# Two transformer blocks on one Trainium2 core: norms summed by token column or inside the next unit's products, a new order of the last two retention heads, and GpSimd multiplying the neighbourhood attention's probabilities

## The reference, cut to what matters

```python
# block 1
x = x + rmsnorm(token_mixer(rmsnorm(x, norm_mix_pre), ...), norm_mix_post)
x = x + rmsnorm(cross_attention(rmsnorm(x, norm_cross_pre), rmsnorm(mem, mem_norm), ...), norm_cross_post)
x = x + rmsnorm(conv_glu_ffn(rmsnorm(x, norm_ffn_pre), ...), norm_ffn_post)
# block 2: an even and an odd layer
x = x + even_mixer(rmsnorm(x, attn_norm_e), ...)   # window attention and neighbourhood attention, 8 heads each
x = x + mlp0(rmsnorm(x, mlp_norm[0]))              # square(relu(h @ w1)) @ w2, width 4096
x = x + odd_mixer(rmsnorm(x, ret_norm_o), ...)     # retention, 8 heads, both directions
x = x + mlp1(rmsnorm(x, mlp_norm[1]))

def rmsnorm(x, g):      # over the 1024 features of each token
    return x * rsqrt(mean(x * x, axis=-1) + 1e-6) * g
# neighbourhood attention, per head and query row
p = softmax(where(valid, q @ k.T * scale + bias, -inf));  o = p @ v
# odd mixer, after retention: per-head group norm, then the gate
y = (silu(g) * groupnorm(y)) @ w_out
```

## Time and profile before

| | |
|---|---|
| median of 3 runs | 2315.23 us (2314.81 to 2315.4) |
| the profiled execution's own time | 2315.41 us |
| its span, first to last instruction | 2313.6 us |
| mean granted TensorE clock | 0.976 of full speed |
| TensorE matmul busy | 2187.5 us, 95% |
| VectorE, ScalarE, GpSimd busy | 1042.4, 854.1, 815.4 us |

### The profile page before, as it was taken

One profiled execution on the slowest core, in us unless ns is written; L12 is line 12 of the kernel. 1 busy time (PEld: TensorE's weight loads), 2 busy tenths in 40 slices (PEclk: granted clock), 3 DMA queues, 4 the chain that ended last, 5 costly groups with the idle time before them and its releaser, 6 DMA issues.

```text
span 2313.6 us, 26996 instructions
## 1 busy us (share of the span) xinstructions
PE 2187.5 (95%) x9972; PEld 1724.4 (75%) x9972; DVE 1042.4 (45%) x1528; ACT 854.1 (37%) x1275; POOL 815.4 (35%) x343
## 2 busy tenths in 40 slices
PE   6889998989999988998999999999999988999999
PEld 5766676758888865765788888788878766888887
DVE  5556646485534363357432312335742665322121
ACT  5334544432222242446442322435432433433231
POOL 3322224224444432220344444443333323444443
PEclk9899999989999999999999999999999999999999
DMA  4212112113322341110222322322222212323223
GB/s 148 66 53 74 64 64 91 64 54 106 123 95 96 100 136 55 64 46 1 83 98 93 100 93 98 107 91 72 75 68 81 80 46 73 97 95 100 95 97 101
DMA packets 54967, 193.36 MB, mean 84 GB/s; under 512 B 6096, under 2 KB 6352, under 8 KB 54480
## 3 DMA queue, kind: packets, MB, share of 16 engines
q1 hardware_dynamic: 50400, 181.58, 24.0%
q10 hardware_dynamic: 4464, 10.36, 1.4%
HBM read 189.82 MB, written 2.10 MB: 83 GB/s over the span
## 4 chain that ended last, share of the span: by engine, by line
PE 73%; issue 13%; DVE 9%; POOL 3%; ACT 2%; DMA 0%; POOLq 0%; SPq 0%; DVEq 0%; ACTq 0%
PE gemm_ps L500 22%; PE gemm_ps L501 21%; PE gemm_ps L502 21%; POOL wl L469 3%; PE out_ps L908 2%; DVE tmp L1654 1%; DVE arena L2022 1%; DVE tmp L2029 1%; PE turn_ps L695 1%; DVE arena L1654 1%; PE score_ps L686 1%; DVE x L1676 1%; PE out_ps L705 1%; DVE xl L1654 1%; PE score_ps L900 1%
## 5 line engine op out<-in xcount | busy, mean ns | idle before, releaser
L469 POOL TENSOR_TENSOR wl<-raw,wh 128x1024 fp32r<-128x1024 f32 x339 | 815.2, 2406 | 1480.4 <-ACT wh L1137 1480.3
L500 PE MATMUL gemm_ps<-xh,wh 128*128 128x512 f32 x1512 | 612.9, 405 | 44.2 <-DVE xl L1654 24.8
L1137 ACT ACTIVATE wh<-raw 128x1024 fp32r<-128x1024 f32 x339 | 359.0, 1059 | 774.5 <-DMA raw<-w_in 745.6
L501 PE MATMUL gemm_ps<-xl,wh 128*128 128x512 f32 x1512 | 593.3, 392 | 0.0
L502 PE MATMUL gemm_ps<-xh,wl 128*128 128x512 f32 x1512 | 593.3, 392 | 0.0
L501 PE MATMUL gemm_ps<-arena_r,wh 128*128 128x512 f32 (+1 forms) x1124 | 433.0, 385 | 0.0
L500 PEld LDWEIGHTS gemm_ps<-xh,wh 128*128 128x128 f32 x1512 | 286.9, 190 | 125.7 <-issue 46.9
L500 PE MATMUL gemm_ps<-arena_r,wh 128*128 128x512 f32 (+1 forms) x868 | 335.5, 387 | 10.8 <-DVE arena_r L1659 10.1
L501 PEld LDWEIGHTS gemm_ps<-xl,wh 128*128 128x128 f32 x1512 | 287.2, 190 | 65.5 <-issue 7.9
L502 PE MATMUL gemm_ps<-arena_r,wl 128*128 128x512 f32 (+1 forms) x868 | 333.3, 384 | 0.0
L502 PEld LDWEIGHTS gemm_ps<-xh,wl 128*128 128x128 f32 x1512 | 286.5, 189 | 61.0
(11 more groups left out here) (334 smaller groups left out, 2011.1 us busy)
## 6 DMA issues: line engine op xcount, KB each, us to landing
raw<-w_in SPq DMA_DIRECT2D x339, 512.0 KB, 3.3
arena<-na_in ACTq DMA_DIRECT2D x14, 256.0 KB, 2.7
x<-x_in SPq DMA_DIRECT2D x8, 256.0 KB, 6.6
out<-x ACTq DMA_DIRECT2D x8, 256.0 KB, 2.8
arena<-alibi_in ACTq DMA_DIRECT2D x6, 256.0 KB, 3.3
con<-con_in SPq DMA_DIRECT2D x1, 1432.0 KB, 11.9
arena<-moba_in ACTq DMA_DIRECT2D x1, 1024.0 KB, 5.1
arena<-mem_in ACTq DMA_DIRECT2D x1, 1024.0 KB, 4.8
```

What stands on the lines that cost most here:

```text
L469: pool.tensor_tensor(wl[:, k, :], raw[:, k, :], wh[:, k, :].bitcast(F32), ALU.subtract).then_inc(unit_split, 1)
L500: pe.matmul(o, wh[:, n % RING, w], h[:, kt, 0:width], start=(kt == 0), stop=False)
L501: pe.matmul(o, wh[:, n % RING, w], l[:, kt, 0:width], start=False, stop=False)
L1137: act.activation(wh[:, k % RING, :], raw[:, k % RING, :], ACT.Copy).then_inc(high_split, 1)
```

## The change

1. *Post-norms by token* (`token_norm`, `inverse_tokens`): the sum of squares goes to 128x4 (token within a tile of 128, by tile), root and reciprocal are taken of 128x4, and four matmuls spread the result over turn_ps bank 1, which `add_normed` now reads in PSUM. For the mixer's and the cross attention's output the last blocks are squared by ScalarE from PSUM, before or beside VectorE's copy.
2. *Pre-norms after an add* (`whole_sum`): the sum stands inside the first unit, after its block kt = 5, and VectorE adds all 8 squares.
3. *Memory units*: `memory_scaled(b)` follows `add_normed` of block b.
4. *Odd order* (`HEAD_STEPS`): the units of heads 6 and 7 are permuted; the last head's two gate units stand beside its own retention steps 0 and 1, head 6's two gate units two places later than head 7's first two. `odd_out1`'s first two units are begun at steps 3 and 4.
5. *Neighbourhood attention*: VectorE stops after the reciprocal; GpSimd multiplies (32 operations), between wl of `even_out`+2 and of `even_out`+3.

```diff
+HEAD_STEPS = [[(h, u) for u in range(U_HEAD)] for h in range(RH - 2)]
+HEAD_STEPS.append([(RH - 2, 0), (RH - 2, 1), (RH - 2, 2), (RH - 2, 3), (RH - 1, 0), (RH - 1, 1)])
+HEAD_STEPS.append([(RH - 1, 2), (RH - 1, 3), (RH - 2, 4), (RH - 2, 5)])
+HEAD_STEPS.append([(RH - 1, 4), (RH - 1, 5)])
+        token_std, token_rstd = eps[:, 4:8], eps[:, 8:12]
+        spread_rstd = turn_ps[:, 1, :]
 # GpSimd
+            beside = FIRST["even_out"] + 3
+            lower_units(0, beside)
+            for i, it in enumerate(pair_items("neighbour")):
+                pool.wait_ge(inverse_ready, i + 1)
+                a = 12 * (i % 3) + 8
+                for s in range(2):
+                    p = pair_probs(i, s, it["nk"], False)
+                    m = pool.tensor_scalar(p, p, small[:, a + s:a + s + 1], None, ALU.mult)
+                m.then_inc(probs_ready, 1)
+            lower_units(beside, UNITS)
 # TensorE
+                    if after is not None and kt == nkt - 3:
+                        after()
+            def whole_sum():
+                take(square_added, KT - 1)
+                pe.matmul(turn_ps[:, 0, :], ones, square_sum, start=True, stop=True).then_inc(square_used, 2)
+            def token_sums(squares, first, last):
+                for c in range(T):
+                    col = CCOL["col"] + 4 - c
+                    m = pe.matmul(turn_ps[:, 0, 0:T], squares[:, c * P:(c + 1) * P], con[:, col:col + T],
+                                  start=(first and c == 0), stop=(last and c == T - 1), skip_group_check=True)
+                return m
+            def token_norm(apart=1):
+                take(square_added, KT - 1 - apart)
+                token_sums(square_sum, True, False)
+                if apart == 2:
+                    take(square_made, KT - 1)
+                    token_sums(sq[:, (KT - 2) % 2, :], False, False)
+                take(square_made, 1 if apart == 2 else KT)
+                token_sums(sq[:, (KT - 1) % 2, :], False, True).then_inc(square_used, 2)
+                take(token_rstd_ready)
+                for c in range(T):
+                    m = pe.matmul(spread_rstd[:, c * P:(c + 1) * P], token_rstd[:, c:c + 1].broadcast_to([P, P]),
+                                  ident, start=True, stop=True)
+                m.then_inc(rstd_spread, 1)
...
-            added_sum()
+            token_norm()              # mixer's and ffn's output; co: token_norm(apart=2)
...
-            added_sum()
-            units(FIRST["mup0"], 1, mh, ml, fresh=True)
+            units(FIRST["mup0"], 1, mh, ml, fresh=True, after=whole_sum)    # ret_unit(0), nup0 alike
...
+                if s < 2:
+                    unit(ret_unit(*HEAD_STEPS[RH][s]), xh, xl)
                 retention(RH - 1, s)
-                for n, at, first, end in ((out1, 0, 0, 6), (out1 + 1, 3, 0, 2), (out1 + 1, 4, 2, 6)):
+                for n, at, first, end in ((out1, 3, 0, 6), (out1 + 1, 4, 0, 6)):
 # ScalarE
+                if tokens:
+                    take(square_used, 2)
+                    act.activation(token_std, turn_ps[:, 0, 0:T], ACT.Sqrt, bias=eps[:, 0:1],
+                                   scale=1.0 / D).then_inc(std_ready, 1)
...
+            prepare(y, None, None, crossed, adds=KT - 3, tokens=True,
+                    banks={KT - 2: score_ps[:, last, :], KT - 1: gemm_ps[:, last, :]})
 # VectorE
+            def inverse_tokens():
+                take(std_ready)
+                done(dve.reciprocal(token_rstd, token_std), token_rstd_ready)
+                take(rstd_spread)
-                stt(tmp[:, b % 2, :], y[:, b, :], p_(post, b), rstd[:, :], ALU.mult, ALU.mult)
+                stt(tmp[:, b % 2, :], y[:, b, :], p_(post, b), spread_rstd, ALU.mult, ALU.mult)
+                    if not scaled_here:
+                        done(dve.reciprocal(part, total), inverse_ready)
+                        return
...
-            inverse()
-            memory_scaled(0)
+            store_one(FIRST["mix"], KT - 1, True)
+            inverse_tokens()
             for b in range(KT):
-                if b < 7:
-                    memory_scaled(b + 1)
                 add_normed("norm_mix_post", "norm_cross_pre", b)
+                memory_scaled(b)
```

More of the change, by code:

```diff
@@ L470, in lower, with lower_units @@
                                    ALU.subtract).then_inc(unit_split, 1)
-            for n in range(RING):
-                lower(n, n + 1)
-            with pool.Fori(1, UNITS // RING) as i:
-                for k in range(RING):
-                    lower(k, RING * i + k + 1)
-            for n in range(UNITS // RING * RING, UNITS):
-                lower(n % RING, n + 1)
+            def lower_units(first, end):
+                n = first
+                while n < min(end, -(-max(first, RING) // RING) * RING):
+                    lower(n % RING, n + 1)
+                    n += 1
+                if end // RING > n // RING:
+                    with pool.Fori(n // RING, end // RING) as i:
+                        for k in range(RING):
+                            lower(k, RING * i + k + 1)
+                    n = end // RING * RING
+                for n in range(n, end):
+                    lower(n % RING, n + 1)
+            beside = FIRST["even_out"] + 3
[8 more added lines that the diff above has]
+            lower_units(beside, UNITS)
         @block.tensor
@@ L491, in meet, with products @@
                 pe.wait_ge(at_dve, meetings[0])
-            def products(n, nkt, h, l, width, fresh=None, summing=False, start=0, summed=0, bank=None):
+            def products(n, nkt, h, l, width, fresh=None, summing=False, start=0, summed=0, bank=None, after=None):
                 o = gemm_ps[:, n % 2 if bank is None else bank, 0:width]
@@ L525, in begun, with units @@
                     pe.matmul(o, wl[:, n % RING, w], h[:, kt, :], start=False, stop=False)
-            def units(n0, count, h, l, nkt=KT, width=N, fresh=False, summing=False, summed=0):
+            def units(n0, count, h, l, nkt=KT, width=N, fresh=False, summing=False, summed=0, after=None):
                 if fresh:
@@ L533, in units @@
                         pe.wait_ge(emptied, n0 - 1)
-                    products(n0, nkt, h, l, width, blocks_split[0], summing, summed=summed)
+                    products(n0, nkt, h, l, width, blocks_split[0], summing, summed=summed, after=after)
                     blocks_split[0] += nkt
@@ L1081, in _ @@
                     if h == 0 and u == 0:
[L1082 to L1084 removed]
+                        units(ret_unit(0), 1, xh, xl, fresh=True, after=whole_sum)
+                    elif u < len(HEAD_STEPS[h]):
+                        unit(ret_unit(*HEAD_STEPS[h][u]), xh, xl)
                     if h:
@@ L1099, in _ @@
             units(out1 + 2, KT - 2, ret_h, ret_l)
-            added_sum()
             take(ret_std)
             take(head_done)
-            units(FIRST["nup0"], 8, xh, xl, fresh=True)
+            units(FIRST["nup0"], 8, xh, xl, fresh=True, after=whole_sum)
             for p in (1, 2, 3):
@@ L1145, in squares, with prepare @@
                 take(square_used, min(2, nb))
-            def prepare(src, gain, h, ready=None, added=False):
+            def prepare(src, gain, h, ready=None, adds=0, tokens=False, banks={}):
                 base = taken.get(square_added, 0)
@@ L1782, in cross_attention, with pair_attention @@
                 take(probs_turned, 3)
-            def pair_attention(items, between=lambda i: None, whole=False, wide=False):
+            def pair_attention(items, between=lambda i: None, whole=False, wide=False, scaled_here=True):
                 def logits(i, it):
```

134 lines of the change are left out of this document (83 added, 51 removed).

## The result

Five runs each, on one chip: before 2315.40 us (2314.81 to 2316.66), changed 2302.16 us (2300.39 to 2303.37). The ratio is 0.9941, with a 95% interval of 0.9927 to 0.9956: faster by 13.2 us. Forecast were 2288.0 us (2278 to 2298) and 27.1 us, so the direction was right and the time lies outside the range. The profiled execution of the changed kernel took 2300.9 us (span 2299.1), 14.5 less than that of before.

What follows compares the result with a forecast made beforehand. TensorE, busy 95% of the span, was taken as the bound, so edits elsewhere count only where it stands still. Terms 10.4 + 6.5 + 2.5 + 6.5 + 4.0 - 2.8 = 27.1 us off 2315.4 gave 2288 us, range 2278 to 2298.

Steps and rivals of the forecast that it cites:

- Neighbourhood attention: Moving its multiplications to GpSimd, at 0.75 us for 384 keys and 0.55 for 256, makes it net 2.8 us slower.
- the 3 that I had counted as given back: Neighbourhood attention's first items, where VectorE is the bound beside the window part's split: about 1 us in three of them.
- Rival D: Neighbourhood attention: GpSimd is dearer than scaled, 1.1 us for 384 keys: +7, total 2292.5 us; chance 0.10.
- The memory loop: Memory units: the period falls from 4.83 to 4.1 us a block; seven turns save 5.2 us.
- rival A: Memory units: the loop keeps its period, 5.2 us less gain, total 2293.5 us; chance 0.12.
- 4.1 against 3.7: Memory loop's period in us: 4.1 if VectorE and GpSimd exclude each other, 3.7 if VectorE is merely slowed.
- The post-norms: Gains of 2.5 us after the feed-forward layer and 6.5 us after the cross attention.
- The sum inside the unit: Sum of squares inside the first unit of mup0, nup0 and the odd layer: together 6.5 us gained (bounds 3.5 to 7.5).
- The odd order: Odd layer's last two heads, units permuted: 4.0 us gained, with VectorE's chain as the bound (bounds 0 and 10.9).
- rival B: Odd layer's retention tail is bound by TensorE, not VectorE: all 10.9 us come, total 2281; chance 0.10.
- The prediction's C: Neighbourhood attention: GpSimd is as quick as VectorE, net -1 us there, total 2284.5; chance 0.10.
- E: Neighbourhood attention: each GpSimd multiplication costs 3 us, hardly depending on width; slower than before, 2335 us; chance 0.03.

Runs made afterwards that it cites:

- one head each: Changed kernel, but VectorE multiplies the first head of each neighbourhood-attention item and GpSimd the second: 2296.76 us, ratio 0.9915 to the kernel before.
- one operation: Changed kernel, but one GpSimd multiplication of two tensors, the inverses broadcast, serves both heads of an item: 2293.91 us, ratio 0.9901 to the kernel before.
- twice: Changed kernel with the neighbourhood attention's multiplications back on VectorE, which does each again by 1.0: 2297.94 us, ratio 0.9916 to the kernel before.
- beside: Changed kernel with VectorE multiplying again, while GpSimd does 32 multiplications of 256 unused columns: 2291.18 us, median of three, ratio 0.9885 to the kernel before.

## Why the prediction was wrong, step by step

**The failed step** is the size of one term, in "Neighbourhood attention": "I take 0.75 and, for 256 keys, 0.55, nearer to GpSimd's own row", with 0.90 for 384 as the bound above. Measured were 1.23 and 0.92. The pair grows by 1.14 us (256: 1.82 and a handover of 0.06, less 0.74) or 1.64 (384), 1.39 in the mean; I had 0.57. By that paragraph's own weights (twelve items at half, four whole: ten times the growth) the right size gives 13.9 us, less the 3 that I had counted as given back, 10.9; measured were 11.9 in the stage and 1.6 behind it. So the size of this one price, with everything else in the sum as it was, accounts for 8.1 of the 10.8 us that the term is off. The weights have no clock in them, which took more than the remaining 2.7: 3.8 us of TensorE's longer instructions in the stage and 1.6 behind it. So they fit only roughly. How much of the 3 us was given back is not measured by itself, and the run with GpSimd for the first four items shows no gain there.

The profiles come near the weights: with the growth at 0.53, 0.51 and 1.39 us (one head each, one operation, the change) the stage lost 4.0, 4.2 and 11.9 us, about 8 for each us where the weights say 10. Where the growth was on VectorE itself (twice: 0.7; beside: 0.25) it was 12.0 and 3.9, about 16; but both figures are from the slowest executions of their versions, and by the medians the five give 15, 10, 10, 13 and 9 us for each us, without such an order. That a place on VectorE is dearer stays open.

**Why the bound was too low.** It scaled a row of another form by columns: the subtraction of two tensors, 2.36 us for 1024. I took a one-input operation to be at most as dear per column as a two-input one. The form with a scalar per partition costs 2.47 ns a column, the one of two tensors with one broadcast 1.68, and wl at most 2.3. The Trainium skill (GPSIMD Engine Reference, section "3.1 Elementwise — side-by-side cycle accounting") gives 769 ns for 512 elements, from which I had an estimate of 0.58 for 384; this case's 1.23 does not agree, and the measurement decides. Both sources said "cheap", and I let them narrow the upper end, where no row of this form stood. Rival D had the mechanism and the sign of the error (1.1 us, +7), at a chance of 0.10; the time came out 10 us beyond it: 6.6 of them in this term (13.6 against its 7), where it too kept the price under the measured one and left out the clock, the rest in the other terms and between median and profile.

**What held.** The memory loop: 4.11 us for 4.1, and rival A is out (0.75 us for the product beside GpSimd in PSUM, 2.83 in SBUF). The Trainium skill's rule (SBUF — State Buffer, section "SBUF: two separate sides"), on which 4.1 against 3.7 hung, agrees with the 2.83. In the neighbourhood attention it does not hold as I took it: a VectorE operation of two tensors beside GpSimd's form with a scalar was stretched from 0.69 to 0.95 and not kept waiting. The post-norms: 2.1 for 2.5 and 5.6 for 6.5, by the handover of 0.5 and by the spread at half clock; they were read from the aligned traces and not undone in a run. The sum inside the unit: 6.1 for 6.5, and 6.3 when undone. The odd order: 3.9 for 4.0 in the aligned traces, but 1 to 2.5 when undone, so right by luck in part; rival B (10.9) is out. The prediction's C (GpSimd as quick as VectorE) and E (3 us whatever the width) are out.

## What to carry to other kernels

An operation moved to another engine is priced by a row of the same form on that engine; where there is none, the range has to reach well past the nearest row (here 1.23 us against the 0.90 scaled from it), and one experiment with that single edit is worth more than the forecast of all others (here 13.5 of 27 us). In a chain over four engines each link's time is part of every item's way, so handing a link to an idle engine lengthens the way if it is slower there; first ask what else the relieved engine would do with the time. And count what a wait costs behind it: ahead of mup0 the sum cost 2.4 us with a matmul inside the wait, and 5.1 without it and with a wait 1.1 us longer, most of the difference in products at the lower clock. Which of the two kept the clock up was not tested.

## What the runs showed of the hardware

- GpSimd, f32: with a scalar per partition 0.92 us for 256 and 1.24 for 384 columns; one operation of two tensors with the scalars broadcast over 512 and 768 columns 1.04 and 1.47.
- In operations of one tensor and a scalar the two engines slow each other. In the run with one head each GpSimd's went from 1.24 to 1.47 and from 0.92 to 1.08, while VectorE's, begun 0.06 us earlier, kept its 0.42 and 0.35. In the run with GpSimd beside, VectorE's went from 0.35 to 0.48 and from 0.42 to 0.54 in the mean, most of it in the first head's, begun 0.05 us earlier than GpSimd's. What decides which of the two is stretched is open.
- A VectorE operation of two tensors in SBUF waited for the end of GpSimd's when that had two tensors too (2.83 beside wl's 2.39; 1.83 instead of 0.69 beside the broadcast form), and was stretched only to 0.95 beside GpSimd's form with a scalar.
- TensorE after 3.3 us of idling: products 0.43 us apart for the next 4 us ahead of mup0 and 6 ahead of nup0, but 0.23 apart from the second on at the odd layer's start. After a wait broken by a matmul pair of 1.02 us, with 1.36 us idle at the end of it: 0.23 from the third product on.
